# Pairing the first two weight blocks behind each norm, waiting for a down product chunk by chunk, and moving conversions ahead of evacuations

## The reference, cut to what matters

```python
def modulate_2(x, gain, shift, scale):
    return rms_norm(x, gain) * (1 + scale) + shift

def swiglu_2(h, w_in, w_out):
    a, b = jnp.split(h @ w_in, 2, axis=-1)      # 1024 -> 2 x 2816
    return (jax.nn.silu(a) * b) @ w_out         # 2816 -> 1024
...
x = x + 0.5 * mod[2] * swiglu_2(modulate_2(x, gain[0], mod[0], mod[1]), ffn_a_in, ffn_a_out)
o = mixer(modulate_2(x, gain[1], mod[3], mod[4]))
x = x + mod[5] * o
x = x + 0.5 * mod[8] * swiglu_2(modulate_2(x, gain[2], mod[6], mod[7]), ffn_b_in, ffn_b_out)
```

## Time and profile before

| | us |
|---|---|
| median of 3 runs (lowest, highest) | 2977.41 (2973.09, 3004.66) |
| span of the profiled execution, first to last instruction | 2968.5 |
| TensorE matmuls busy | 2538.3 (86%), 13974 matmuls |
| VectorE busy | 1711.2 (58%) |
| ScalarE busy | 865.2 (29%) |
| mean granted clock of TensorE | 0.915 of full |

### The profile page before, as it was taken

How to read it: one execution, slowest core, us unless ns; L and a number is a source line. 1 busy time by engine, 2 the same in 40 slices (tenths; PEclk the granted TensorE clock), 3 DMA queues, 4 the chain that set the end, 5 groups by cost and what they waited for, 6 DMA issues and landing times.

```text
span 2968.5 us, 38026 instructions
## 1 busy us (share of the span) xinstructions
PE 2538.3 (86%) x13974; PEld 2151.4 (72%) x13974; DVE 1711.2 (58%) x2629; ACT 865.2 (29%) x1052; POOL 83.1 (3%) x106
## 2 busy tenths in 40 slices
PE   3997766888799997964768999989999889968898
PEld 1997745888588786842447887768887679957898
DVE  5776644884788766687436888243332253355554
ACT  0443323433322222112303222223222131323443
POOL 0000000000000000000001000000000000000000
PEclk6999867999899998976689999999999999989999
DMA  5677521665255443430002554222222232301444
GB/s 201 232 257 261 209 99 42 220 223 174 105 198 193 167 161 116 157 113 25 32 0 85 198 198 170 88 96 85 99 90 83 103 113 87 140 28 57 153 176 153
DMA packets 79450, 399.81 MB, mean 135 GB/s; under 512 B 8672, under 2 KB 12512, under 8 KB 54176
## 3 DMA queue, kind: packets, MB, share of 16 engines
q1 hardware_dynamic: 78176, 393.84, 37.6%
q0 software_dynamic: 1216, 5.24, 0.5%
HBM read 396.95 MB, written 2.10 MB: 134 GB/s over the span
## 4 chain that ended last, share of the span: by engine, by line
PE 70%; DVE 14%; issue 6%; DMA 5%; ACT 4%; SPq 0%; DVEq 0%; ACTq 0%; POOL 0%; POOLq 0%
PE pg L664 19%; PE pg L666 19%; PE pg L665 19%; DMA raw<-w_t 2%; DMA raw<-w_d 2%; DVE ada L1014 2%; PE pg L809 2%; PE px L787 1%; PE pg L727 1%; PE pg L726 1%; PE pg L725 1%; ACT whi L426 1%; ACT whi L431 1%; DMA ada<-w_ada 1%; DVE RS L1132 1%
## 5 line engine op out<-in xcount | busy, mean ns | idle before, releaser
L664 PE MATMUL pg<-Yh,whi 128*128 128x256 f32 (+1 forms) x2912 | 981.6, 337 | 128.6 <-DVE Yl L1142 92.7
L665 PE MATMUL pg<-Yl,whi 128*128 128x256 f32 (+1 forms) x2912 | 974.7, 335 | 0.0
L666 PE MATMUL pg<-Yh,wlo 128*128 128x256 f32 (+1 forms) x2912 | 974.0, 334 | 0.0
L992 DVE TENSOR_TENSOR wlo<-raw,whi 128x2048 fp32r<-128x2048 f32 (+1 forms) x228 | 474.5, 2081 | 587.8 <-ACT whi L431 587.0
L664 PEld LDWEIGHTS pg<-Yh,whi 128*128 128x128 f32 x2912 | 560.6, 193 | 195.8 <-issue 114.0
L431 ACT ACTIVATE whi<-raw 128x2048 fp32r<-128x2048 f32 (+1 forms) x228 | 398.2, 1747 | 773.2 <-PE pg L666 658.4
L665 PEld LDWEIGHTS pg<-Yl,whi 128*128 128x128 f32 x2912 | 561.0, 193 | 52.7
L666 PEld LDWEIGHTS pg<-Yh,wlo 128*128 128x128 f32 x2912 | 560.3, 192 | 53.3
L664 PE MATMUL pg<-Hh,whi 128*128 128x256 f32 (+1 forms) x1056 | 360.2, 341 | 34.8 <-DVE Hl L1076 28.4
L665 PE MATMUL pg<-Hl,whi 128*128 128x256 f32 (+1 forms) x1056 | 357.9, 339 | 0.0
L666 PE MATMUL pg<-Hh,wlo 128*128 128x256 f32 (+1 forms) x1056 | 357.6, 339 | 0.0
(11 more groups left out here) (201 smaller groups left out, 1995.7 us busy)
## 6 DMA issues: line engine op xcount, KB each, us to landing
raw<-w_t SPq DMA_DIRECT2D x194, 1024.0 KB, 4.8
ada<-w_ada SPq DMA_DIRECT2D x216, 512.0 KB, 3.3
raw<-w_d SPq DMA_DIRECT2D x96, 704.0 KB, 4.0
NB<-na_bias POOLq DMA_DIRECT2D x8, 256.0 KB, 2.9
X<-x_t SPq DMA_DIRECT2D x1, 1024.0 KB, 8.5
spectrum<-HF POOLq DMA_DIRECT2D x1, 1024.0 KB, 4.9
X<-ctx_t SPq DMA_DIRECT2D x1, 1024.0 KB, 7.2
DF<-dft POOLq DMA_DIRECT2D x1, 1024.0 KB, 5.0
```

What stands on the lines that cost most here:

```text
L664: pe.matmul(out, w_hi, y_hi, start=first, stop=False)
L665: pe.matmul(out, w_hi, y_lo, start=False, stop=False)
L666: return pe.matmul(out, w_lo, y_hi, start=False, stop=last)
L992: dve.tensor_tensor(wlo[:, n % 2, 0:size], raw[:, n % 2, 0:size], whi[:, n % 2, 0:size].bitcast(F32), ALU.subtract)\
```

## The change

1. For the ten phases in `READS`, TensorE takes blocks 0 and 1 together: per chunk `kt` it multiplies both blocks, 12 matmuls instead of 6, in two PSUM buffers. Both blocks must be converted first. The loop over the rest of the phase starts with block 2.
2. The wait for all 22 hidden chunks ahead of a down product is gone. Inside the product, the first of each two output chunks waits for 11 chunks at the first half's start, 20 at the second half's, 21 and 22 at the last two `kt`.
3. In the last iteration of every phase, `ahead` converts first and evacuates after that, on ACT and DVE, as in the loop.
4. With `defer`, only the last conversion is left to the norm (`second`); the next phase's block 0 is now converted in `ahead`, ahead of the last evacuation.
5. On ACT, the table with the square root is loaded by an instruction of its own behind the squares, ahead of `second`.

```diff
@@ ACT, ahead (DVE the same with lo_static)
                         if last:
+                            n = base + u + 2 + per * j
+                            if size_of(n) and not (defer and u == per - 1):
+                                hi_static(n, size_of(n))
                             evac(j, u)
-                            n = base + u + 2 + per * j
-                            if size_of(n) and not (defer and u >= per - 2):
-                                hi_static(n, size_of(n))
@@ ACT
+            def second(name):
+
+                hi_static(BASE[name] + 1, size_of(BASE[name] + 1))
@@ ACT, norm (DVE: second in place of first_two, ahead of the reciprocal)
+                act.preload_act_table(ACT.Sqrt)
                 if following:
-                    first_two(following)
+                    second(following)
@@ TensorE, product, mode "d"
+                    h_before = KF * [f.replace("gu", "down") for f in FFNS].index(name) + CREDIT
                     with pe.Fori(0, blocks // 4) as j:
...
+                                    if v == 0 and (half, kt) in ((0, 0), (1, 0), (1, 9), (1, 10)):
+                                        pe.wait_ge(sem["h_lo"], h_before + (11 if half == 0 else 20 if kt == 0 else 12 + kt))
@@ TensorE, product, mode "t"
+                paired = 1 if name in READS and mode == "t" else 0
+                if paired:
                     for u in range(2):
+                        pe.wait_ge(sem[evac], ebase + u - 2 + 1)
+                        pe.wait_ge(sem["lo_ready"], base + u + CREDIT + 1)
+                    for kt in range(8):
+                        pe.wait_ge(sem["y_lo"], y_before(READS[name]) + kt + 1)
+                        for u in range(2):
+                            for half in range(2):
+                                w = slice(256 * kt + P * half, 256 * kt + P * half + P)
+                                last = three(pg[u][:, half, 0:tokens], whi[:, u, w], wlo[:, u, w],
+                                             Yh8[:, kt, 0:tokens], Yl8[:, kt, 0:tokens], kt == 0, kt == 7)
+                            if kt == 7:
+                                last.then_inc(sem["pe_block"], 1)
+                with pe.Fori(0, blocks // 2 - paired) as j:
...
@@ TensorE, ffn
                 product(f"{blockname}_gu{i + 1}")
-                pe.wait_ge(sem["h_lo"], KF * (FFNS.index(f"{blockname}_gu{i + 1}") + 1) + CREDIT)
                 product(f"{blockname}_down{i + 1}")
```

More of the change, by code:

```diff
@@ L419, in first_two @@
                 for n in (BASE[name], BASE[name] + 1):
-                    if size_of(n):
-                        hi_static(n, size_of(n))
+                    hi_static(n, size_of(n))
+            def second(name):
+                hi_static(BASE[name] + 1, size_of(BASE[name] + 1))
             def hi_static(n, size):
@@ L696, in product @@
                     return
-                with pe.Fori(0, blocks // 2) as j:
+                paired = 1 if name in READS and mode == "t" else 0
+                if paired:
                     for u in range(2):
-                        pe.wait_ge(sem[evac], j * 2 + (ebase + u - 2 + 1))
-                        pe.wait_ge(sem["lo_ready"], j * 2 + (base + u + CREDIT + 1))
+                        pe.wait_ge(sem[evac], ebase + u - 2 + 1)
[10 more added lines that the diff above has]
+                with pe.Fori(0, blocks // 2 - paired) as j:
+                    for u in range(2):
+                        pe.wait_ge(sem[evac], j * 2 + (ebase + 2 * paired + u - 2 + 1))
+                        pe.wait_ge(sem["lo_ready"], j * 2 + (base + 2 * paired + u + CREDIT + 1))
                         if mode == "t":
                             for kt in range(8):
-                                if u == 0 and name in READS:
-                                    pe.wait_ge(sem["y_lo"], y_before(READS[name]) + kt + 1)
                                 for half in range(2):
@@ L1047, in body @@
                         if last:
+                            n = base + u + 2 + per * j
+                            if size_of(n) and not (defer and u == per - 1):
+                                lo_static(n, size_of(n))
                             evac(j, u)
-                            n = base + u + 2 + per * j
-                            if size_of(n) and not (defer and u >= per - 2):
-                                lo_static(n, size_of(n))
                         else:
@@ L1059, in first_two, with second @@
                 for n in (BASE[name], BASE[name] + 1):
-                    if size_of(n):
-                        lo_static(n, size_of(n))
+                    lo_static(n, size_of(n))
+            def second(name):
+                lo_static(BASE[name] + 1, size_of(BASE[name] + 1))
             def nothing(j, u):
```

## The result

The changed kernel takes 3036.3 us (median of 4 executions, 3020.87 to 3048.13) against 2978.69 (4, 2973.09 to 3004.66); the ratio is 1.0182, with a 95% interval of 1.0140 to 1.0224. That is 54 us more by the ratio. The four executions fall into two pairs, 3021 and 3026, 3046 and 3048, and the median lies between them, where no execution is. The profiled one is the slowest (3048.13); its span is 3046.4, 77.9 above the span before.

The account below looks back on a forecast made before the run. TensorE, with 70% of the chain of waits, was taken to bound the kernel. The terms -27 + 30.2 + 8 - 4.8 + 17.6 + 13.9 gave +37.9 on 2977.4, so 3015 us, range 2985 to 3036.

Parts of the forecast that it names:

- Part 2, -27: Six down products: removing the wait for 22 hidden chunks gains 27 us with the clock, bounds 18 and 35.
- point (1): Sign in the profile after: `Hl` no longer stands in TensorE's waits with more than 5 us.
- Part 1's stalls, 30.2 + 2.8: TensorE idle behind pairs: eight pairs lose 30.2 us, `b1_qk`'s 2.8 is counted with the mixer, `l1_q` costs nothing.
- The clock behind a pair, 8: Behind eight pairs' waits of about 4 us: low clock costs 0 to 13 us, 8 taken.
- Rival A: Behind pairs: every wait drops the clock, 3024 us, or it holds, 3007; chance within the forecast's shared 0.64.
- Part 4, -4.8 and +17.6: Norms: one conversion less gains 4.8 us in five; ahead of `b1_qk`, `l0_qk`, `l1_q` late blocks lose 17.6.
- Part 3, +13.9, "elsewhere nothing": Phase ends: conversion ahead of evacuation loses 13.9 us at `b1_gelu`, `l0` key norm and `l1_g`, nothing elsewhere.

Follow-up runs that it names:

- part 2 alone: Kernel before, with TensorE waiting for the hidden chunks inside the down product: 2955.8 us, ratio 0.9930.
- the pair alone: Kernel before, with only blocks 0 and 1 side by side behind each norm, 12 matmuls a chunk: 3035.6 us, ratio 1.0195.
- the lag of four chunks: Kernel before with blocks 0 and 1 paired, but block 1 following block 0 four chunks behind: 2988.1 us, ratio 1.0027.
- the change with the extra matmuls: Changed kernel plus 24 matmuls with unused results in front of the first window head's transposes in l0's attention: 3026.2 us, ratio 1.0140.
- part 4 alone: Kernel before, with only the last conversion left in the norm and the table load, evacuation still ahead of conversion: 2996.9 us, ratio 1.0059.
- the kernel before with the extra matmuls: Kernel before plus 24 matmuls with unused results ahead of the second head's scores in l0's attention: 2981.0 us, ratio 0.9998.

## Why the prediction was right or wrong

The direction was right and the size short: 3015 was forecast with an upper end of 3036, and the median is 3036.3, on that end; by the ratio it is 3032. That it came so near is in part luck, for the median depends on how many of four executions had the attention at the lower clock. Between the two profiles the count is cleaner. Without the attention's 25 us they are 53 apart, where the sum had 38: the pairs' stalls and clock 53.5 (forecast 41), the six down products -29.1 (-27), the norms +17.4 and -2.5 (+17.6 and -4.8), and the waits at the three boundaries +8.3 (11.1 without the pair's 2.8), together 47.6. The 5 us that are left were not put down to a place. Going through its steps:

- **Part 2, -27.** Right: -23 in the median of the part alone, -24.7 over the six down products of its profile, and -29.1 over those of the changed kernel (597.6 to 568.5). The `Hl` wait is gone, as point (1) said.
- **Part 1's stalls, 30.2 + 2.8.** The mechanism is shown, by the pair alone and by the lag of four chunks; each stall has nearly the size worked out (4.2 and 3.8 forecast, 4.03 and 3.65 measured in `b1_gu1` and `l0_gu1`). `l1_q` is right in an odd way: it shows a wait of 4.78, but block 2 starts 18.1 us after the first chunk and started 18.3 after it before, so only the clock behind it costs. Without it 35.9 us of idle time stand where I had 33; the difference is 1.4 us over the eight pairs, for which I had credited up to 0.7 each that the pair didn't give back, and 1.5 in `b1_qk`, which has the full 4.3.
- **The clock behind a pair, 8.** This is the term that was mis-sized. I read the level from the first matmul after a wait and put the waits of 2.26 and 2.73 us down as harmless. That sign is no good, because the level can fall some way into the work. Stretches of the kernel before, behind the wait of 2.73 us:

```profile
356.50:358.40 1.90, 1.82 (x14) 1.83 (x15) 1.90 (x2) 0.65 (x1) 0.00 (x0) 0.93 0.87 291
358.40:361.40 3.00, 3.00 (x16) 3.00 (x16) 2.75 (x7) 0.00 (x0) 0.00 (x0) 0.50 0.86 345
```

The first 1.9 us are at 0.93, the next 3 at 0.50: this wait had cost the level too, and my middle between 2.7 and 7.6 us rested on a misread row. All ten waits of 3.65 to 4.78 lost it, 1.4 to 2.6 us each, 17.6 in all: 13.6 behind the eight pairs for which the sum had 8, just over its bound of 13, and 4.0 behind `b1_qk` and `l1_q`, for which it had no such term. Rival A had this right in kind, with 13 for the eight. The Trainium skill (TensorE: Matmul & The Clock Gate, section HAM oscillation — how this bites in real kernels) tells of the same fall, at the wait for a transfer ahead of every one of a kernel's bursts of matmuls. Here the waits were for VectorE, and the trace agrees in every pair (0.61 granted in the 4 us behind two of the stalls, as shown). The stalls without `l1_q`'s and the clock come to 53.5 us (35.9 and 17.6), most of the 57 that the pair alone measured.
- **Part 4, -4.8 and +17.6.** Right for the three late norms: 17.4 to 17.5 (5.3, 7.5 and 4.6 in the changed kernel; forecast 5.5, 7.5, 4.6). The gain in the five others was smaller than forecast, 3.6 us alone and 2.5 in the changed kernel, and `b1_2` gained nothing.
- **Part 3, +13.9, "elsewhere nothing".** The three boundaries cost 9.6 alone (11.1 forecast without the pair) and `b1_v` 1.3, and the other places nothing only because part 2 is there too. Alone the part costs 28 to 32, since the last hidden chunk comes later in six FFNs and the whole product waited for it. The forecast used this cover without naming it, and what it costs when it is gone: 16 us.
- **What was missing.** The level of TensorE's clock in the `l0` attention, 25 us in an execution that has the lower one. It does not need the change: by their times the kernel before has it in 5 of 25 executions, part 2 alone in 4 of 10, the changed kernel in 2 of 4, and the change with the extra matmuls in none of 4. Whether the change makes it more frequent stays open. The profiles give a hint that it does, through part 2. In the six without part 2 the level rose 8 to 10 us behind the first head's reciprocal. Of the six with it, those with matmuls directly in front of the heads left out, one was like these (9 us), and in the other five it rose 20 to 72 us behind. No run was made to test this.

The range was too narrow at the top by the same two: the clock's term belonged at its bound, and the attention's level was a bound of its own. The times of the kernel before, up to 3004.66, were a sign of it.

## What to carry to other kernels

Two blocks that are multiplied side by side also end side by side, and with two weight buffers nothing is then left to cover the next conversion: the price is one conversion less the distance between the two ends, plus the clock's fall behind it (here 1.4 to 2.8 us a pair). A step that is put ahead of another on an in-order engine costs what its own input is late, so ask for each place whether its transfer is early; the same edit gained 3.8 us in four norms, nothing in a fifth, and cost 17.5 in three. Parts of a change don't add where one removes the wait in which another would show: here they gave -23, +18 and +32 singly and nothing together.

## What the runs showed of the hardware

- What a wait of TensorE does to the level need not show in the first matmul behind it. The level fell 1.5 us into the work behind a wait of 2.73 us, and between 2.0 us before and 0.9 us into the work behind the ten pairs' waits of 3.65 to 4.78 us. Shorter waits went either way in the same place: after 2.26 or 2.27 us in front of `b1_down1` the level stayed in two profiles (before, part 4 alone) and fell in three (the pair alone, the pair with the lag, the kernel before with the extra matmuls); after 3.07 to 3.10 us in front of `l1_down1` it stayed in three and fell in two. Waits of 1.15 to 1.91 us behind the pairs with the lag cost it nowhere.
- One stretch of a program can run at either level of the clock. The window heads, chains of small matmuls with short waits, began at 0.50 in all twelve profiles without matmuls directly in front of them. The level rose 8 to 10 us behind the first head's reciprocal in seven, 20 behind it in one, 62 in two, and 72, behind the last head, in two. The same 125 matmuls took 61 us at the one level and 36 at the other, and TensorE was busier at the low level (54.3 of 61 us) than at the high one (28.9 of 36), without the clock rising. Under nine us of unbroken matmuls directly in front the level rose in both profiles and stayed, and all 10 executions lay in the lower group by their times; the same matmuls 7 us earlier raised it too, and it fell again in the wait behind them.
- Loading the root's table took 1.28 us and was done straight ahead of the next ACT instruction, with no further delay around it.
